# Gate rows' thirty transposes and four spreading products dealt out between the passes of the third and fourth values tiles

## The reference, cut to what matters

```python
mq, mk, mv, mo, mg, aq, ak, av, bg = jnp.split(h @ w_in, idx, axis=-1)
...
mg = mg.reshape(B, T, 2, 2, M_HEADS).astype(f32) + gate_bias.astype(f32)
...
def step(carry, inp):
    C, n, m = carry
    qc, kc, vc, fc, ic = inp
    b = jnp.cumsum(fc, axis=-1)
    dmat = jnp.where(lower, b[..., :, None] - b[..., None, :] + ic[..., None, :], -jnp.inf)
    inter = b + m[..., None]
    m_t = jnp.maximum(inter, jnp.max(dmat, axis=-1))
    ...
    g = b_last[..., None] - b + ic
    m_new = jnp.maximum(b_last + m, jnp.max(g, axis=-1))
    a_prev = jnp.exp(b_last + m - m_new)
    kw = kc * jnp.exp(g - m_new[..., None])[..., None]
    C_new = a_prev[..., None, None] * C + jnp.einsum("bhsd,bhse->bhde", kw, vc)
```

## Time and profile before

| | us |
|---|---|
| median of 3 runs | 1714.87 |
| lowest, highest | 1714.63, 1716.12 |
| span of the profiled execution | 1715.9 |
| TensorE (PE) busy | 1695.8 |
| TensorE weight loads (PEld) busy | 1564.3 |
| VectorE (DVE) busy | 1046.0 |
| ScalarE (ACT) busy | 688.1 |
| mean granted TensorE clock | 0.997 |

### The profile page before, as it was taken

How to read it: one execution, slowest core, us unless ns; L and a number is a source line. 1 busy time by engine, 2 the same in 40 slices (tenths; PEclk the granted TensorE clock), 3 DMA queues, 4 the chain that set the end, 5 groups by cost and what they waited for, 6 DMA issues and landing times.

```text
span 1715.9 us, 28055 instructions
## 1 busy us (share of the span) xinstructions
PE 1695.8 (99%) x11327; PEld 1564.3 (91%) x11327; DVE 1046.0 (61%) x1777; ACT 688.1 (40%) x1254; POOL 0.2 (0%) x4
## 2 busy tenths in 40 slices
PE   8999999999999999999999999999999999999998
PEld 6999899989979989999999888889989988998997
DVE  5756465666465314555536877775646844982885
ACT  6322222212364322344355554553474433541453
POOL 0000000000000000000000000000000000000000
PEclk9999999999999999999999999999999999999999
DMA  9435443433314224332342311101521221222233
GB/s 387 174 135 217 139 159 135 156 139 123 90 59 160 74 62 104 85 97 80 86 150 81 113 53 41 41 27 64 209 75 73 81 93 61 97 89 86 74 99 148
DMA packets 58651, 189.50 MB, mean 110 GB/s; under 512 B 7672, under 2 KB 16680, under 8 KB 56744
## 3 DMA queue, kind: packets, MB, share of 16 engines
q1 hardware_dynamic: 58536, 187.89, 32.7%
HBM read 170.67 MB, written 16.54 MB: 109 GB/s over the span
## 4 chain that ended last, share of the span: by engine, by line
PE 91%; DVE 3%; ACT 3%; issue 1%; DMA 0%; DVEq 0%; SPq 0%; ACTq 0%
PE psum L709 13%; PE psum L710 12%; PE psum L711 12%; PE psum L812 4%; PE psum L691 4%; PE psum L693 4%; PE psum L814 4%; PE psum L692 4%; PE psum L813 4%; PE psum L1233 2%; PE psum L1215 2%; PE psum L782 2%; PE psum L783 2%; PE psum L781 2%; PE psum L1193 2%; PE psum L1118 1%
## 5 line engine op out<-in xcount | busy, mean ns | idle before, releaser
L1866 DVE TENSOR_TENSOR wlo<-raw,whi 128x1024 fp32r<-128x1024 f32 x148 | 181.2, 1224 | 370.4 <-ACT whi L1327 370.3
L1327 ACT CAST whi<-raw 128x1024 fp32r<-128x1024 f32 x148 | 155.1, 1048 | 325.0 <-PE psum L814 140.7
L709 PE MATMUL psum<-h_hi,whi 128*128 128x320 f32 x720 | 223.8, 311 | 0.0
L711 PE MATMUL psum<-h_hi,wlo 128*128 128x320 f32 x720 | 222.5, 309 | 0.0
L710 PE MATMUL psum<-h_lo,whi 128*128 128x320 f32 x720 | 222.4, 309 | 0.0
L709 PE MATMUL psum<-g_hi,whi 128*128 128x320 f32 x656 | 209.4, 319 | 0.2 <-ACT gate L1684 0.2
L711 PE MATMUL psum<-g_hi,wlo 128*128 128x320 f32 x656 | 202.7, 309 | 0.0
L710 PE MATMUL psum<-g_lo,whi 128*128 128x320 f32 x656 | 202.6, 309 | 0.0
L709 PEld LDWEIGHTS psum<-h_hi,whi 128*128 128x128 f32 x720 | 135.1, 188 | 4.6 <-issue 4.5
L710 PEld LDWEIGHTS psum<-h_lo,whi 128*128 128x128 f32 x720 | 135.2, 188 | 0.0
L711 PEld LDWEIGHTS psum<-h_hi,wlo 128*128 128x128 f32 x720 | 135.1, 188 | 0.0
(11 more groups left out here) (442 smaller groups left out, 3733.1 us busy)
## 6 DMA issues: line engine op xcount, KB each, us to landing
raw<-in_w_ffn_in SPq DMA_DIRECT2D x88, 512.0 KB, 3.6
raw<-in_w_mix SPq DMA_DIRECT2D x77, 512.0 KB, 4.1
raw<-in_w_ffn_out SPq DMA_DIRECT2D x44, 512.0 KB, 3.5
mw<-in_w_mod SPq DMA_DIRECT2D x28, 768.0 KB, 5.1
mw<-in_w_mod SPq DMA_DIRECT2D x8, 1024.0 KB, 16.1
gate<-gate_keep SPq DMA_DIRECT2D x24, 320.0 KB, 4.9
mw<-in_w_mod SPq DMA_DIRECT2D x14, 512.0 KB, 4.5
gate_keep<-gate SPq DMA_DIRECT2D x20, 320.0 KB, 4.7
```

The costliest lines, as they stand in the source:

```text
L709: mm(out, wh[:, k, :], hi[:, k, cols], start=(k == 0), stop=False)
L711: last = mm(out, wl[:, k, :], hi[:, k, cols], start=False, stop=(k == nk - 1))
L1327: copy((to or whi[t.slot])[:, :, :], raw[t.raw][:, :, :]).then_inc(w_hi, 1)
L1866: tt(lo[:, :, :], raw[t.raw][:, :, :], hi[:, :, :].bitcast(F32), ALU.subtract).then_inc(raw_free, 1)
```

## The change

The thirty transposes are no longer one block behind tile v = 2. They are dealt out inside it: before each of its ten passes stands a group of three (`gi`, `gf` and `gm` of one block and direction). The four spreading products stand singly before the first four passes of tile v = 3. `take_gates` moves on VectorE from the step l = 11 to the step l = 12. The waits for the rows go to the first group.

```diff
+GATE_V = 2
...
                         for c in range(NT):
                             if v % 4 == 0 and o == 0:
                                 bank_free(c)
+                            if v == GATE_V:
+                                turn_gates(o * NT + c)
                             last = passes(c, o)
...
                     for n, c in enumerate(MV_LAST[f]):
                         for o in range(2):
+                            if v == GATE_V + 1 and 2 * n + o < 4:
+                                spread_decays(2 * n + o)
                             last = passes(c, o)
...
-            def turn_gates():
-                pe.wait_ge(row_a, 6)
-                pe.wait_ge(row_d, ROW_END)
+            def turn_gates(n):
+                c, d = n // 2, n % 2
+                if n == 0:
+                    pe.wait_ge(tr_ev, 3)
+                    pe.wait_ge(row_a, 6)
+                    pe.wait_ge(row_d, ROW_END)
                 for q, src in enumerate((gi, gf, gm)):
-                    for c in range(NT):
-                        for d in range(2):
-                            o = ((q * NT + c) * 2 + d) * H
-                            last = tp(psum[:, 5, o:o + H], src[:, d, c * P:(c + 1) * P], ident[0:H, 0:H])
-                last.then_inc(tok_t, 1)
...
+                    o = ((q * NT + c) * 2 + d) * H
+                    last = tp(psum[:, 5, o:o + H], src[:, d, c * P:(c + 1) * P], ident[0:H, 0:H])
+                if n == 2 * NT - 1:
+                    last.then_inc(tok_t, 1)
+
+            def spread_decays(j):
+                if j == 0:
+                    pe.wait_ge(sel_in, 3)
+                last = mm(psum[:, 5, (24 + j) * 2 * NT:(25 + j) * 2 * NT], sel2[0:H, j, :].bitcast(F32),
+                          ar[:, :, :].rearrange("h d c -> h (d c)"), start=True, stop=True)
+                if j == 3:
+                    last.then_inc(tok_t, 1)
...
-                if l == L_MK + 6:
-                    pe.wait_ge(tr_ev, 3)
-                    turn_gates()
             half_gemm(0)
...
-                if l == L_MK + 6:
+                if l == L_MV + GATE_V + 1:
                     take_gates()
```

More of the change, by code:

```diff
@@ L1030, in turn @@
                 last.then_inc(tr_done, 1)
-            def turn_gates():
-                pe.wait_ge(row_a, 6)
-                pe.wait_ge(row_d, ROW_END)
-                for q, src in enumerate((gi, gf, gm)):
-                    for c in range(NT):
-                        for d in range(2):
-                            o = ((q * NT + c) * 2 + d) * H
-                            last = tp(psum[:, 5, o:o + H], src[:, d, c * P:(c + 1) * P], ident[0:H, 0:H])
-                last.then_inc(tok_t, 1)
[L1041 to L1045, removed]
+            def turn_gates(n):
[4 more added lines that the diff above has]
+                    pe.wait_ge(row_d, ROW_END)
+                for q, src in enumerate((gi, gf, gm)):
+                    o = ((q * NT + c) * 2 + d) * H
[9 more added lines that the diff above has]
+                    last.then_inc(tok_t, 1)
             first_four(0, T_MIX)
```

## The result

| | before | after |
|---|---|---|
| median of the timed runs, us | 1715.49 (4 runs, 1714.63 to 1716.27) | 1724.14 (4 runs, 1723.58 to 1725.11) |
| ratio after / before | | 1.005, 95% interval 1.0038 to 1.0062 |
| span of the profiled execution, us | 1715.9 | 1721.9 |
| time of the profiled execution, us | not taken | 1723.69 |
| mean granted clock in it | 0.997 | 0.999 |

The change makes the kernel 8.65 us slower, 0.50%. The forecast was 4.3 us slower, with a range that ended at 1721.3. The direction, the wait and the low clock behind it were forecast rightly. So the size was half of what came.

The account below looks back on a forecast made before the run. The prediction took TensorE's stream to bound the kernel. From the median: 1714.87 - 5.2 (gates before) + 3.9 (dealt-out work) + 3.9 (wait) + 1.7 (clock) = 1719.2 us, +0.25%, range 1716.4 to 1721.3.

Parts of the forecast that it names:

- The bound: TensorE is busy 1695.8 of 1715.9 us, so a microsecond it loses or saves mid-program is about one of the kernel.
- The wait: At the seventh product of tile v = 4, TensorE stalls 3.80 us for VectorE's copies, plus 0.11 in the first step.
- The clock after the wait: Large products behind the stall in tile v = 4 run at a low clock: 1.7 us, bounds 0 and 3.4.
- The clock holds in tiles v = 2 and 3: With small work dealt out between large products, the clock should stay at 2.4 GHz in these tiles.
- The dealt-out work: Ten transpose groups in tile v = 2 and four spreading products in v = 3 cost 3.9 us (2.2 to 5.4).
- the prediction's own sign of being wrong: Groups over 0.4 us each; also idle time missing or under 2 us, or a clock fall within tile v = 2.
- Rival 2: Weight loads hide beside large products: groups cost 0.12, spreads 0.26, 2.2 us in all, total 1717.5; chance 0.13.
- What the gates cost before: Block behind tile v = 2 takes 3.51 us, low clock in v = 3 2.70: 6.21 together, 5.2 against the median.
- 1: The wait in tile v = 4 comes but TensorE's clock holds at 2.4 GHz: 1717.5 us; chance 0.15.
- 3: The copies finish early enough that tile v = 4 has no stall: 1713.6 us, 1712 with rival 2; chance 0.05.
- Rival 4: Seams on both sides, groups 0.36 and spreads 0.45, or a full low-clock stretch: 1720.7 us; chance 0.17.

Follow-up runs that it names:

- e6: The changed kernel with sixteen repeated large products at the head of tile v = 4, filling TensorE's wait: 1721.36 us, ratio 1.0031 to before.
- e2: The kernel before with its block of small products left in place and only VectorE's two copies out of bank 5 moved later: 1720.80 us, ratio 1.0026.
- e3: The kernel before without the thirty transposes and four spreading products, one f32 product of 300 columns in their place: 1711.70 us, ratio 0.9976.
- e8: As e4, with the four spreading products in one block before the first pass of tile v = 3: 1714.75 us, ratio 0.9995 to before.
- e9: As e8, with all thirty transposes in one group before the sixth pass of tile v = 2: 1715.44 us, ratio 1.0000 to before.
- e4: The changed kernel with the copies out of bank 5 early and the transposes in two groups of fifteen: 1715.41 us, ratio 1.0001 to before.

## Why the prediction was right on the wait and wrong on the dealt-out work

**The bound.** TensorE's stream sets the time: right. What the runs put into it or took out of it moved the total by as much to within 1.2 us (the ledger), and the sixteen products of e6 that filled idle time cost nothing.

**The wait.** Forecast 3.80 and 0.11; measured 3.74 and 0.11, at the product named, with VectorE's four instructions in the order and at the distances read from the earlier trace rows. Right. e2 shows it alone.

**The clock after the wait.** Forecast 1.7; 1.6 in the trace, 2.8 by e6 in the median. Right in kind; the timed runs may lose more. The rule of the Trainium skill, "TensorE: Matmul & The Clock Gate", section "Loop structure matters more than you think", that products behind a long wait run cold, held here with a delay: the first 1.4 us of products behind the wait still ran at 1.00, and the next 3.4 us at 0.50. With the same wait filled by products (e6) the clock stays up. The clock holds in tiles v = 2 and 3: right.

**The dealt-out work.** This is the first step that failed, and the one that turned a gain into a loss. The term was 0.25 a group and 0.35 a spreading product, 3.9 in all with 5.4 as the upper end; it measured 0.49 and 0.53, 7.0 in all. Ten groups over 0.4 us each were the prediction's own sign of being wrong, and with 1.17 us instead of 0.95 from pass to pass it came. The choice was to put the seam at one side only, by the earlier trace rows, and to give part of it back for a first load hidden beside a large product. The trace shows that load unhidden. And the earlier trace rows hid more than one seam: there the large product starts 0.03 us after the last transpose (579.93 to 579.96), here 0.13 after it, and there the load of the first transpose begins with the product before, at 579.35. Transposes of 128 columns were not a fair stand-in for ones of 8. Even the upper end, "both seams", left the step from the last small product to the large one out. Rival 2 was wrong: by it a group would cost 0.12, and it costs four times that. The Trainium skill, "TensorE: Matmul & The Clock Gate", section "Step-by-step: what each phase is for", says that weight loads are pulled ahead of running matmuls under two conditions; the trace agrees between large products (0.22 us ahead) and shows none of it at either seam of a group.

**What the gates cost before.** The second step that failed. The 6.21 us were read correctly, but from an execution that is not like the timed ones. I set its span, 1715.9, against the median time, 1714.87, and took them to be 1.0 apart. A span leaves out what lies around it: in the profiled run after, 1723.69 - 1721.9 = 1.8 us, and the runs of before show 1.7 to 1.8 as well. So the profiled execution of before took about 1717.7 by this estimate, 2.2 to 2.8 over the medians, and more of the 6.21 was clock that the median does not lose. By e3 the block costs the median 3.0 + 1.5 = 4.5 us.

**The sum again.** Against the profiled execution: -6.2 + 7.0 + 3.85 + 1.6 = +6.2, where the spans differ by 6.0. Against the median: -4.5 + 7.0 + 3.85 + 1.6 = +8.0, where 8.65 was measured. The forecast loss was 4.3 us short: 3.1 are the dealt-out work and 0.7 the price before (5.2 taken, 4.5 found), less 0.2 for a wait and a clock taken slightly too high; 0.7 stay open, as in the ledger.

**The rivals.** 1 and 3 did not come. Rival 2 was answered above. Rival 4 named "seams on both sides" and came nearest, with 1720.7; its 1.5 us for them is half of the 3.1 that came. The measured 1724.14 lies outside every rival.

## What to carry to other kernels

Small products between large ones had a fixed price per detour here that was larger than the work of three of them: count how often TensorE goes in and out, and read the price of a detour from products of the same shape. One large block had the lower price but a clock that sometimes fell; the best arrangement found (e8) is not distinguishable from before. When a step is moved to a later place in an in-order queue, look for what now stands ahead of it that only starts when a tile ends: two copies that take 0.5 us together, put behind two other instructions, cost 3.8 us of TensorE and a low clock on top. Before a profiled execution is used as the base of a sum, add what lies around its span and compare its mean clock with the timed runs.

## What the runs showed of the hardware

- A detour between products of 128 x 512 into transposes of 8 columns costs 0.30 us beside 0.062 per transpose: 0.10 to enter, 0.02 more in the first small step, 0.07 more from the last small one to the large one, 0.11 in the first large step. It fits groups of three and of fifteen (594.86 to 595.98 and 0.11 in e8's trace is 1.23).
- In e9's trace the clock fell to 1.2 GHz 1.2 us after a group of thirty such transposes, 2 us long, though large products had resumed; behind groups of fifteen, 1 us long, it stayed at 1.00 in the traces of e4 and e8. Behind the block of the kernel before, the low stretch lasted 6.8 us in one trace and 3.4 in that of e2. The timed runs of before spread over 5 us, and those with a lower mean clock are the longer ones.
- After an idle time of 3.6 us the clock was still 1.00 for the first 1.4 us of new products in after and for 0.6 us in e2 (from 617.74 to about 618.36), and then stood at 0.50 for 3.4 us in both: the price comes later than its cause.
- A weight load for products of 128 x 512 begins 0.22 us ahead of its product, beside the one before; the first load on either side of a group of small transposes began within 0.01 us of its own product.
